# Head sums of the squared differential queries and keys: one plain fp32 matmul each, or two matmuls of a rounded and a low part

## The chip, the cores and the metric

The kernel runs on one core of a Trainium2 chip. The metric is the device time of one execution in microseconds, the median of several runs. TensorE (PE) does the matmuls, VectorE (DVE), ScalarE (ACT) and GpSimd (POOL) the elementwise work; SyncE (SP) starts most of the DMAs. Every engine works through its own list in a fixed order and waits on semaphores.

## What is computed

Two transformer blocks follow each other on a sequence of 512 tokens of width 1024. The change lies in the second block, in its differential attention. There queries and keys are normalised head by head before the scores:

```python
q, k, v = jnp.split(z.astype(F32), 3, axis=-1)
q = rms_normalize(q.reshape(B, S, H, 2, DIFF_QK)) * q_norm.astype(F32)
k = rms_normalize(k.reshape(B, S, H, 2, DIFF_QK)) * k_norm.astype(F32)
```

`rms_normalize` divides by the root of the mean of the squares over the 64 elements of a half head (plus 1e-6). Queries and keys together are 1024 columns: eight tiles of 128 columns by 512 tokens, with two half heads in each tile. In the same block stand a pooling mixer, an RWKV-7 mixer, then an output projection, a cross attention and a gated FFN.

## The kernel before, in words

Activations lie transposed, features on the partitions and the 512 tokens along the free axis. Every large projection is written as three matmuls in a rounded format (fp32r): ACT rounds the weights of a chunk of 256 output columns to a high part (L1192, one instruction of 128x2048 per chunk), POOL subtracts to get the low part (L2499, four instructions of 128x512), and PE adds high x high, high x low and low x high (`mm3`, eight contraction steps, so 24 matmuls for a tile of 128x512). The activations are split in the same way into `h_high_low` and `h_low`. The constants lie in `consts`; `blk` there is a 128x128 matrix with 1/64 in its two diagonal 64x64 blocks, so that a matmul with it gives each row the mean over its half head.

The stage around the change treats eight tiles t = 0 to 7 (`dq`, four of queries and four of keys). For each tile:

- PE projects it (`project("dq", ...)`) into a bank of PSUM.
- DVE multiplies by the token scale and writes it to `dqk`, which is `xres` (`dq_out`, L2095).
- ACT squares it into `qk_sq`, one of two buffers in `sums` (`dq_square`, L1579).
- PE forms the means, `dq_sum(t)`, through the helper `block_sum`: one plain fp32 matmul of 128x512 with `blk`. The profile shows a plain fp32 matmul as two instructions ("x2"), so the four for two tiles read "banks<-sums,consts ... x4".
- ACT takes Ln and Exp(-0.5 x) of it (`dq_inverse`, L1585 and L1587). From t = 2 on it first waits until the DVE has scaled tile t - 2, which used the same buffer (`dqk_ready` at least t - 1).
- DVE multiplies by gain and inverse (`dqk_scaled`, L2168), which counts `dqk_ready` up.

Each engine's order is written out by hand. PE: dq 0 to 3 with other small sums between (kk, pool, bonus), sums 0 and 1, dq 4, sums 2 and 3, dq 5, sum 4, dq 6, sum 5, dq 7, sum 6, sixteen transposes (nat 0, into four banks), sum 7, sixteen transposes (nat 1), then the value projection `dv` (128x256 tiles). All of these results pass through a ring of four banks, and `take` waits until the former tile of a bank has been moved out. DVE: `dq_out(3)`, two products from PSUM (`bonus`, L2178), `decayed(0)` (six operations, L2114 to L2120), `dq_out(4)`, `dqk_scaled` 0 and 1, `decayed(1)` (the same six lines), `dq_out(5)`, `dqk_scaled(2)`, `dq_out(6)`, `dqk_scaled(3)`, `dq_out(7)`, `dqk_scaled` 4 to 7. ACT: after `dq_square(7)` it does `dq_inverse(6)`, moves the four nat 0 banks (L1238), does `dq_inverse(7)` and moves the four nat 1 banks. Rounding the weights of the first `dv` chunk (L1192) stands behind `dq_square(5)`.

The means over all features of a token (`norm_sum`) and the sums kk and bonus are plain fp32 matmuls as well and are not touched. `nF_rows` (tile `forget_rows`) and `masks` hold data of the first block's attention; `nF_rows` is used again for the differential attention's outputs later.

Of the kernel before, what the change touches and what calls it, by code (L numbers as in the profile page):

```python
# [8 lines left out]
F32R = mybir.dt.float32r  # L9
BF16 = mybir.dt.bfloat16  # L10
ACT = mybir.ActivationFunctionType
ALU = mybir.AluOpType

P = 128
# [129 lines left out]
def build(nc, x_in, mem_in, params_in, consts_in, ada_in, stream_in, with_f_in, down_in, out, x2_kept, kx_kept, vx_kept, nF_kept, sums_kept):  # L144
    with ExitStack() as ctx:
# [3 lines left out]
        def sem(name):  # L149
            if name not in sems:  # L150
                sems[name] = ctx.enter_context(nc.semaphore(name))
            return sems[name]
# [62 lines left out]
        def sb(name, *dims, kind=F32):  # L215
            n = int(np.prod(dims))
            return view(ctx.enter_context(nc.sbuf_tensor(name, [P, n], kind))[:, :], dims)
# [13 lines left out]
        xres = sb("xres", KD, T)  # L231
        h_raw, h_lo = sb_both("h", KD, T)
        h_high, h_hi = sb_both("h_high", KD, T)
        sums = sb("sums", 4, T)
        sq, acc, rms = sums[:, 0:2, :], sums[:, 2, :], sums[:, 3, :]
        mod = sb("mod", 24)
        gmod = sb("gmod", 8)
        gmix = sb("gmix", 8)
        small = sb("small", 64)
        dq8 = sb("dq8", 2)  # L240
        masks = sb("masks", 3, P, kind=BF16)
        nF_rows = sb("forget_rows", 2, T)

        with nc.sbuf_tensor("arena", [P, ARENA], F32) as arena:
            pass
# [66 lines left out]
        POOL_W = PAD + T  # L312
        ycat03 = at(5152, 4, T)
        dqk = xres
        qk_sq, qk_rinv = sq, [acc, rms]
        zscale, rms2 = at(23456, T), sq[:, 1, :]

        dv, dist = zm[:, 0:4, :], zm[:, 4:8, :]
# [165 lines left out]
        def _(pe):  # L484
# [304 lines left out]
            def block_sum(key, j, src, ready):  # L789
                pe.wait_ge(sem(ready), j + 1)  # L790
                o = M.take(pe, (key, j))
                mm(o, blk, src, True, True, M.filled)

            def dq_sum(t):
                block_sum("dn", t, qk_sq[:, t % 2, :], "qk_squares")

            project("zr", 1, KD, h, T, first=5)
            rates(0)
# [360 lines left out]
        def _(act):  # L1159
# [13 lines left out]
            def split_weights(part=0, parts=1):  # L1173


                c = chunks[0]
                if part == parts - 1:
                    chunks[0] += 1
                if c >= STREAM:
                    down_high(c - STREAM)  # L1180
                    return
                n = width_of(c) // parts
                cols = slice(n * part, n * (part + 1))
                if part == 0:
                    act.wait_ge(*loaded_of(c))
                    if hi_holder(c) is not None:
                        end = chunk_end[hi_holder(c)]
                        if end[0] == "used":
                            act.wait_ge(used[end[1]], end[2])
                        else:  # L1190
                            full(end)
                nc.scalar.activation(hi_of(c)[:, cols], raw_of(c)[:, cols], ACT.Copy)\  # L1192
                    .then_inc(sem("weights_hi"), PIECES // parts)
# [324 lines left out]
            squares(3, xres, T, lambda k: act.wait_ge(sem("x2_ready"), k + 1))  # L1518

            act.dma_start(x2_kept, xres).then_inc(sem("x2_stored"), 16)  # L1520
            split_weights()
            inverse_rms(3, T, rms2)

# [51 lines left out]
            def dq_square(t):  # L1575
                if t >= 2:
                    M.full(act, ("dn", t - 2))
                M.wait_out(act, ("dq", t))
                nc.scalar.activation(qk_sq[:, t % 2, :], dqk[:, t, :], ACT.Square).then_inc(sem("qk_squares"), 1)  # L1579

            def dq_inverse(t):
                o = M.full(act, ("dn", t))
# [248 lines left out]
        def _(dve):  # L1831
# [280 lines left out]
            def decayed(j):  # L2112
                dve.wait_ge(sem("kk_norm"), j + 1)
                link(tt(adec[j], adec[j], tB[j], ALU.mult))  # L2114
                link(tt(bdec[j], avec[j], adec[j], ALU.mult))
                dve.wait_ge(sem("exps"), 4 * j + 4)
                tt(rdec[j], rdec[j], zm[:, j, :], ALU.mult).then_inc(sem("decayed"), 1)
                tt(bdec[j], bdec[j], kdec[j], ALU.mult).then_inc(sem("decayed"), 1)
                tt(kdec[j], kdec[j], kvec[j], ALU.mult).then_inc(sem("decayed"), 1)
                stt(adec[j], adec[j], -1.0, decay[j], ALU.mult, ALU.mult).then_inc(sem("decayed"), 1)  # L2120
# [22 lines left out]
            def dq_out(t):  # L2143
                token_scaled(("dq", t), dqk[:, t, :])

            inv_count = con("inv_count", 2, T)
            for j in range(2):
# [14 lines left out]
                    ins = tt(d, d, u[rows, PAD:], ALU.subtract)  # L2162
                ins.then_inc(sem("pooled"), 1)

            def dqk_scaled(t):
                dve.wait_ge(sem("qk_inverse"), t + 1)
                g = dq8[:, 0:1] if t < 4 else par("dk_g")
                stt(dqk[:, t, :], dqk[:, t, :], g, qk_rinv[t % 2], ALU.mult, ALU.mult).then_inc(sem("dqk_ready"), 1)  # L2168

            dq_out(1)  # L2170
            for j in range(2):
                o = M.full(dve, ("kk", j))
                ts(tB[j], o, float(HEAD), 1e-24, ALU.mult, ALU.max).then_inc(M.out(("kk", j)), 1)
            dq_out(2)
            dq_out(3)
            for j in range(2):
                o = M.full(dve, ("bonus", j))
                stt(bonus[j], o, float(HEAD), zm[:, 4 + j, :], ALU.mult, ALU.mult).then_inc(M.out(("bonus", j)), 1)  # L2178
            decayed(0)
            dq_out(4)  # L2180
            dqk_scaled(0)
            dqk_scaled(1)
            decayed(1)
            dq_out(5)
            dqk_scaled(2)
            dq_out(6)
            dqk_scaled(3)
            dq_out(7)
            for t in range(4, 8):
                dqk_scaled(t)  # L2190

# [551 lines left out]
```

## Time and profile before

| | |
|---|---|
| median of 3 runs | 1288.5 us (1288.05 to 1291.14) |
| the profiled execution | 1291.47 us, span from first to last instruction 1289.7 us |
| PE busy | 1253.3 us, 97% of the span |
| DVE, ACT, POOL busy | 699.2, 568.5 and 530.7 us |
| mean granted TensorE clock | 0.997 |
| stage of the change | about 582 to 642 us of the span |

How to read it: times are microseconds from the span's start. A row of a timeline has the start, the duration, the engine and line, the operation, the tiles it writes and reads, how many instructions are merged, and in brackets how long the engine was idle before and what released it. A merged row's duration runs from the first start to the last end. Matmuls are pipelined, so a fp32r matmul of 128x512 is shown with 0.39 or 0.40 us although the next one starts 0.23 us later; the pace is read from the starts.

### The profile page before, as it was taken

What the parts mean: (1) busy time and instruction counts of PE and PEld (TensorE: products, weight loads), DVE (VectorE), ACT (ScalarE), POOL (GpSimd) and SP (SyncE); (2) the same over time, 40 slices, a digit from 0 to 9 for tenths busy, and PEclk for the clock granted to TensorE, in tenths of its full rate; (3) what the DMA queues carried; (4) which work ended last, traced back from release to release, by engine and by line L of the source; (5) the groups of instructions that cost most, each with busy time, mean ns of one, the idle gap of its engine ahead of it and who ended that gap; (6) DMA issues with size and microseconds to landing.
All of it is one profiled execution on the core that took longest, in us unless ns stands there. A gap on an engine that the chain in (4) does not pass through costs nothing.

```text
span 1289.7 us, 20794 instructions
## 1 busy us (share of the span) xinstructions
PE 1253.3 (97%) x8570; PEld 1019.5 (79%) x8570; DVE 699.2 (54%) x1093; ACT 568.5 (44%) x870; POOL 530.7 (41%) x424
## 2 busy tenths in 40 slices
PE   6999999999999999999998899999999999999999
PEld 5788888866678888767786767788788888888999
DVE  3250004886431266686557657265565665766773
ACT  6541444786665233354544544353422221224452
POOL 6544454322234544534242126331444444546321
PEclk9999999999999999999999999999999999999999
DMA  9836795612115452412220013310222222224554
GB/s 387 348 131 243 248 230 191 163 50 97 51 66 188 122 163 79 181 66 76 69 107 16 3 66 131 135 61 34 99 98 98 81 87 94 99 88 172 166 185 151
DMA packets 24907, 165.05 MB, mean 128 GB/s; under 512 B 2792, under 2 KB 2920, under 8 KB 11504
## 3 DMA queue, kind: packets, MB, share of 16 engines
q1 hardware_dynamic: 20448, 128.15, 27.9%
q10 hardware_dynamic: 2064, 24.07, 5.0%
q0 software_dynamic: 2304, 11.54, 4.5%
q8 instruction: 68, 1.11, 0.3%
q14 instruction: 23, 0.19, 0.0%
HBM read 157.43 MB, written 29.38 MB: 145 GB/s over the span
## 4 chain that ended last, share of the span: by engine, by line
PE 89%; DVE 4%; ACT 3%; POOL 2%; issue 1%; DMA 0%; SPq 0%; DVEq 0%; ACTq 0%
PE banks L488 87%; PE banks L495 2%; DVE arena L1985 1%; POOL h_low L2557 1%; DVE arena L1982 1%; DVE arena L1987 1%; POOL weights_low L2557 1%; DMA arena<-in_mem 0%; ACT weights_high L1192 0%; ACT arena L1238 0%; ACT memory_high L1248 0%; ACT arena L1416 0%; ACT arena L1417 0%; ACT arena L1415 0%; DVE arena L1943 0%
## 5 line engine op out<-in xcount | busy, mean ns | idle before, releaser
L2499 POOL TENSOR_TENSOR weights_low<-weights,weights_high 128x512 fp32r<-128x512 f32 x324 | 433.2, 1367 | 580.5 <-ACT weights_high L1192 580.5
L488 PE MATMUL banks<-h_high_low,weights_high 128*128 128x512 f32 x880 | 358.2, 407 | 1.6 <-ACT arena L1443 1.6
L488 PE MATMUL banks<-h_low,weights_high 128*128 128x512 f32 x880 | 348.9, 397 | 0.0
L488 PE MATMUL banks<-h_high_low,weights_low 128*128 128x512 f32 x880 | 348.8, 396 | 0.0
L1192 ACT ACTIVATE weights_high<-weights 128x2048 fp32r<-128x2048 f32 (+2 forms) x90 | 156.3, 1737 | 243.1 <-PE banks L488 226.0
L488 PEld LDWEIGHTS banks<-h_high_low,weights_high 128*128 128x128 f32 x880 | 166.0, 189 | 46.0 <-issue 5.8
L488 PEld LDWEIGHTS banks<-h_low,weights_high 128*128 128x128 f32 x880 | 166.0, 189 | 41.8 <-issue 3.6
L488 PEld LDWEIGHTS banks<-h_high_low,weights_low 128*128 128x128 f32 x880 | 165.8, 188 | 40.4
L488 PE MATMUL banks<-arena 64*64 64x64 f32 (+6 forms) x1800 | 118.1, 263 | 4.1 <-issue 2.6
L488 PEld LDWEIGHTS banks<-arena 64*64 64x64 f32 (+3 forms) x1800 | 85.9, 148 | 29.9 <-issue 23.2
L1238 ACT ACTIVATE arena<-banks 128x256 f32<-128x256 f32 (+4 forms) x82 | 41.9, 519 | 53.4 <-PE banks L495 35.1
L2411 DVE TENSOR_TENSOR arena<-banks,sums 128x512 f32<-128x512 f32 x22 | 15.2, 692 | 78.1 <-PE banks L488 73.0
L488 PE MATMUL banks<-t_high,weights_low 128*128 128x256 f32 x198 | 55.6, 281 | 0.0
L488 PE MATMUL banks<-weights_high,h_high_low 128*128 128x256 f32 (+1 forms) x192 | 55.3, 288 | 0.3 <-ACT arena L1238 0.3
L488 PE MATMUL banks<-weights_high,h_low 128*128 128x256 f32 (+1 forms) x192 | 54.2, 282 | 0.0
L488 PE MATMUL banks<-weights_low,h_high_low 128*128 128x256 f32 (+1 forms) x192 | 54.1, 282 | 0.0
L1221 ACT ACTIVATE sums<-xres 128x512 f32<-128x512 f32 x32 | 20.2, 631 | 70.3 <-DVE xres L2065 39.3
L1938 DVE COPY arena<-banks 128x256 f32<-128x256 f32 (+3 forms) x40 | 25.3, 632 | 47.1 <-PE banks L488 46.2
L488 PE MATMUL banks<-t_high,weights_high 128*128 128x256 f32 x154 | 43.5, 283 | 2.5 <-issue 1.5
L488 PE MATMUL banks<-t_high,h_high_low 128*128 128x256 f32 x154 | 42.7, 277 | 0.0
L2557 POOL TENSOR_TENSOR weights_low<-weights,weights_high 128x384 fp32r<-128x384 f32 (+1 forms) x20 | 21.3, 1094 | 47.3 <-ACT weights_high L1202 47.3
L495 PE MATMUL banks<-consts,arena 128*128 128x128 f32 x245 | 37.2, 277 | 1.6 <-DVE arena L2222 0.8
(360 smaller groups left out, 2371.9 us busy)
## 6 DMA issues: line engine op xcount, KB each, us to landing
weights<-in_stream SPq DMA_DIRECT2D x82, 1024.0 KB, 4.8
sums_kept<-in_down POOLq DMA_DIRECT2D x16, 704.0 KB, 12.8
arena<-in_ada SPq DMA_DIRECT2D x8, 1024.0 KB, 11.9
weights<-in_down SPq DMA_DIRECT2D x9, 704.0 KB, 4.1
weights<-sums_kept SPq DMA_DIRECT2D x9, 704.0 KB, 4.0
sums_kept<-in_down ACTq DMA_DIRECT2D x2, 2816.0 KB, 21.4
sums_kept<-sums_kept ACTq DMA_DIRECT2D x2, 2816.0 KB, 12.6
h<-sums_kept SPq DMA_DIRECT2D x7, 704.0 KB, 4.2
```

The source lines that it names most:

```text
L488: ins = nc.tensor.matmul(o, lhsT, rhs, start=start, stop=stop, skip_group_check=skip)
L495: ins = nc.tensor.transpose(o, i, ident[0:rows, 0:rows])
L1192: nc.scalar.activation(hi_of(c)[:, cols], raw_of(c)[:, cols], ACT.Copy)\
L1221: nc.scalar.activation(SQ[n][i % 2][:, 0:width], src[:, k, 0:width], ACT.Square)\
L1238: nc.scalar.activation(dst, s_, ACT.Copy).then_inc(ring_.out(key), 1)
L1938: nc.vector.tensor_copy(dst, o if src is None else src(o)).then_inc(ring_.out(key), 1)
L1982: link(stt(w, o[:, :, 0:end], 0.0, w, ALU.max, ALU.add))
L1985: ins = nc.vector.tensor_tensor_scan(v, ones(end), v, 0.0, ALU.mult, ALU.add)
L1987: tt(w, o[:, :, 0:end], w, ALU.subtract).then_inc(M2.out(("a", i)), 1)
L2411: tt(a[:, 2:T + 2], o, rms[:, :], ALU.mult).then_inc(M.out(("up", m, 0)), 1)
L2499: nc.gpsimd.tensor_tensor(lo_of(c)[:, cols], raw_of(c)[:, cols], hi_of(c)[:, cols].bitcast(F32), ALU.subtract).then_inc(sem("weights_split ...
L2557: nc.gpsimd.tensor_tensor(down_lo(i)[:, cols], down_raw(i)[:, cols], down_hi(i)[:, cols].bitcast(F32), ALU.subtract).then_inc(sem("down_lo ...
```

## The change

Each square is taken twice by ACT: once in fp32 (`qk_sq`) and once rounded to fp32r (`qk_hi`, in `nF_rows`). DVE subtracts the rounded one from the full one (`square_low`, writing `qk_lo` over `qk_sq`), and PE adds two fp32r matmuls with a fp32r copy of `blk` (`blk_r`, in the place of `masks`). `dq_sum` now waits for `qk_low`. Where the DVE does its eight subtractions is part of the diff. ACT makes `blk_r` once, between the second block's first norm and the next rounding of weights.

```diff
-        sums = sb("sums", 4, T)
+        sums, sums_r = sb_both("sums", 4, T)
...
-        masks = sb("masks", 3, P, kind=BF16)
-        nF_rows = sb("forget_rows", 2, T)
+        with nc.sbuf_tensor("masks", [P, 3 * P], BF16) as held:
+            pass
+        masks, blk_r = view(held[:, :], (3, P)), sb("blocks", 3 * P // 2, kind=F32R)[:, 0:P]
+        nF_rows, nF_rows_r = sb_both("forget_rows", 2, T)
...
-        qk_sq, qk_rinv = sq, [acc, rms]
+        qk_sq, qk_lo, qk_hi, qk_rinv = sq, sums_r[:, 0:2, :], nF_rows_r, [acc, rms]
...
+            pe.wait_ge(sem("blocks"), 1)
+
             def dq_sum(t):
-                block_sum("dn", t, qk_sq[:, t % 2, :], "qk_squares")
+                pe.wait_ge(sem("qk_low"), t + 1)
+                o = M.take(pe, ("dn", t))
+                mm(o, blk_r, qk_hi[:, t % 2, :], True, False)
+                mm(o, blk_r, qk_lo[:, t % 2, :], False, True, M.filled)
...
             act.dma_start(x2_kept, xres).then_inc(sem("x2_stored"), 16)
+            high(blk_r, blk, sem("blocks"))
             split_weights()
...
                 nc.scalar.activation(qk_sq[:, t % 2, :], dqk[:, t, :], ACT.Square).then_inc(sem("qk_squares"), 1)
+                nc.scalar.activation(qk_hi[:, t % 2, :], dqk[:, t, :], ACT.Square).then_inc(sem("qk_squares"), 1)
...
+            def square_low(t):
+                dve.wait_ge(sem("qk_squares"), 2 * t + 2)
+                low(qk_lo[:, t % 2, :], qk_sq[:, t % 2, :], qk_hi[:, t % 2, :], sem("qk_low"))
...
             dq_out(2)
+            square_low(0)
             dq_out(3)
+            square_low(1)
             for j in range(2):
                 o = M.full(dve, ("bonus", j))
                 stt(bonus[j], o, float(HEAD), zm[:, 4 + j, :], ALU.mult, ALU.mult).then_inc(M.out(("bonus", j)), 1)
             decayed(0)
+            square_low(2)
             dq_out(4)
+            square_low(3)
             dqk_scaled(0)
             dqk_scaled(1)
             decayed(1)
+            square_low(4)
             dq_out(5)
             dqk_scaled(2)
+            square_low(5)
             dq_out(6)
             dqk_scaled(3)
+            square_low(6)
             dq_out(7)
+            square_low(7)
             for t in range(4, 8):
                 dqk_scaled(t)
```

## Rows read from the trace of the kernel before

**Rows 1.** The page: span, TensorE's busy time, shares of the chain that ended last.
```profile
span 1289.7 us, 20794 instructions
PE 1253.3 (97%) x8570; PEld 1019.5 (79%) x8570; DVE 699.2 (54%) x1093; ACT 568.5 (44%) x870; POOL 530.7 (41%) x424
...
PE 89%; DVE 4%; ACT 3%; POOL 2%; issue 1%; DMA 0%; SPq 0%; DVEq 0%; ACTq 0%
```
**Rows 2.** Timeline of PE around sums 0 to 3 and dq 4.
```profile
607.96 1.88 PE L488 MATMUL banks<-sums,consts 128*128 128x512 f32 x4
...
609.91 0.39 PE L488 MATMUL banks<-h_low,weights_high 128*128 128x512 f32 x1
...
615.29 1.88 PE L488 MATMUL banks<-sums,consts 128*128 128x512 f32 x4
...
617.24 0.40 PE L488 MATMUL banks<-h_low,weights_high 128*128 128x512 f32 x1
```
**Rows 3.** ACT's rows of the stage: two squares, then tile 7 and the bank moves.
```profile
611.51 1.14 ACT L1579 ACTIVATE sums<-xres 128x512 f32<-128x512 f32 x2
...
636.54 0.63 ACT L1579 ACTIVATE sums<-xres 128x512 f32<-128x512 f32 x1 [3.39 <-DVE xres L2095]
637.20 0.69 ACT L1585 ACTIVATE sums<-banks,consts 128x512 f32<-128x512 f32 x1
...
638.46 2.04 ACT L1238 ACTIVATE arena<-banks 128x512 f32<-128x512 f32 x4
```
**Rows 4.** Instructions of `low` and `high` (min/median/max ns, first and last start).
```profile
L1855 DVE TENSOR_TENSOR gated_low<-arena,gated_high_a x4: 681/684/686, 390.0 to 391.8; 128x512 fp32r<-128x512 f32 x4
...
L1211 ACT ACTIVATE masks<-consts x3: 304/308/309, 78.5 to 78.9; 128x128 bf16<-128x128 f32 x3
```
**Rows 5.** Timeline of DVE, from `dq_out(3)` to `dq_out(4)`.
```profile
606.44 0.69 DVE L2095 TENSOR_TENSOR xres<-banks,arena 128x512 f32<-128x512 f32 x1 [6.64 <-PE banks L488]
...
608.16 0.69 DVE L2178 SCALAR_TENSOR_TENSOR arena<-banks,arena 128x512 f32<-128x512 f32 x1 [0.17 <-PE banks L488]
608.77 1.55 DVE L2114 TENSOR_TENSOR arena<-arena 128x512 f32<-128x512 f32 x1
...
615.95 0.68 DVE L2120 SCALAR_TENSOR_TENSOR arena<-arena 128x512 f32<-128x512 f32 x1
616.55 0.68 DVE L2095 TENSOR_TENSOR xres<-banks,arena 128x512 f32<-128x512 f32 x1
```
**Rows 6.** Timeline of POOL from 608 to 617 us.
```profile
608.51 6.37 POOL L2499 TENSOR_TENSOR weights_low<-weights,weights_high 128x512 fp32r<-128x512 f32 x4 [9.61 <-ACT weights_high L1192]
```
**Rows 7.** Timeline of PE from sum 6 to the first matmul of `dv`.
```profile
635.55 1.02 PE L488 MATMUL banks<-sums,consts 128*128 128x512 f32 x2
636.41 2.18 PE L495 MATMUL banks<-consts,arena 128*128 128x128 f32 x16
639.18 1.10 PE L488 MATMUL banks<-sums,consts 128*128 128x512 f32 x2 [0.58 <-ACT arena L1238]
640.11 1.91 PE L495 MATMUL banks<-consts,arena 128*128 128x128 f32 x16
642.27 0.39 PE L488 MATMUL banks<-weights_high,h_high_low 128*128 128x256 f32 x1 [0.25 <-ACT arena L1238]
```
**Rows 8.** Timeline of DVE, scaling of tile 6 (`dqk_scaled(6)`).
```profile
638.58 0.75 DVE L2168 SCALAR_TENSOR_TENSOR xres<-xres,params,sums 128x512 f32<-128x512 f32 x1 [0.81 <-ACT sums L1587]
```
**Rows 9.** Busy time and granted clock (the number behind POOL) by stretch.
```profile
548.00:552.00 4.00, 1.09 (x6) 0.33 (x4) 3.85 (x7) 3.04 (x5) 0.00 (x0) 1.00 0.00 0
552.00:556.00 4.00, 4.00 (x9) 2.17 (x8) 3.84 (x6) 3.33 (x6) 0.00 (x0) 0.57 0.01 4
673.00:677.00 4.00, 2.39 (x76) 2.01 (x74) 2.48 (x9) 3.86 (x9) 1.26 (x1) 1.00 0.53 168
677.00:681.00 4.00, 3.70 (x182) 3.17 (x183) 3.47 (x9) 1.12 (x3) 0.89 (x1) 1.00 0.26 102
743.00:747.00 4.00, 4.00 (x18) 2.30 (x18) 3.49 (x5) 0.96 (x3) 3.65 (x3) 0.57 0.66 205
```

## The prediction

> **What bounds the kernel now.** I read the page first, then the timelines of PE, DVE, POOL and ACT for the stage of the change, and last the granted clock. PE is busy for 97% of the span and carries 89% of the chain that ended last [rows 1]. So a microsecond taken from PE's list is worth a microsecond, and a microsecond in which PE waits costs one. In the timelines the reader is to see two places of this stage where another engine runs beside PE with little or no slack: the DVE in `decayed(0)`, and ACT between tile 7's square and the bank moves.
>
> **What the change removes.** Sums 0 and 1 start at 607.96 us, and the second matmul of dq 4 starts at 609.91 us: 1.95 us for two sums and one fp32r matmul [rows 2]. The 23 fp32r matmuls from 609.91 to 615.29 us take 5.38 us, 0.234 us each. So a plain sum costs (1.95 - 0.23) / 2 = 0.86 us, and two fp32r matmuls of the same size cost 0.47 us. The saving is 0.39 us for a sum, 3.1 us for eight. If nothing else moved, this would be the gain.
>
> **What it adds and where that lies.** ACT gets eight more squares at a pace of 0.52 us (two take 1.14 us, one alone 0.63 [rows 3]). DVE gets eight subtractions; the same helper on the same shape and types takes 0.68 us [rows 4], at DVE's pace of 0.60 us from start to start [rows 5]. Both engines are idle for almost half of the kernel, so their busy time is nothing. What matters is that `dq_sum(t)` now stands behind a DVE instruction, in DVE's fixed order.
>
> *Sums 0 and 1.* `square_low(0)` waits only for ACT and is over before dq 3 ends. `square_low(1)` follows `dq_out(3)` at 606.44 us and ends near 607.8 us; PE wants it at 608.4 us. No wait. It pushes the products behind it by up to 0.6 us, but the second one waited for PE until 608.16 anyway [rows 5], so `decayed(0)` starts about 0.1 us later. PE gains 2 x 0.39: dq 4 starts 0.8 us earlier and ends at 615.29 - 0.77 = 614.5 us.
>
> *Sums 2 and 3.* This is the first stall. `square_low(2)` stands behind `decayed(0)`. That begins at 608.77 us and its last operation starts at 615.95 us; `dq_out(4)` follows at 616.55 us, not because PE was late (dq 4 ended at 615.3) but because the DVE was busy [rows 2, 5]. The reason is visible beside it: POOL's weight subtractions run from 608.51 us for 6.37 us [rows 6], and the first operation of `decayed(0)` takes 1.55 us, where the last takes 0.68 us [rows 5]. So `square_low(2)` starts at 616.65 us and ends at 617.35 us; PE, ready at 614.5 us, stands still for 2.9 us. Then sum 2 (0.47 us, to 617.9), while the DVE does `dq_out(4)` (from 617.25) and `square_low(3)` (617.86 to 618.56). PE waits another 0.7 us, does sum 3 and starts dq 5 at 619.1 us. Before, dq 5 started at 617.24 - 0.23 = 617.0 us [rows 2]. At this point the change has lost 2.1 us, the saving of four sums included.
>
> The Trainium skill ("SBUF — State Buffer", section "Who interferes with whom") says that a DVE instruction with two SBUF inputs contends with a GpSimd instruction that reads SBUF and that the loser waits for the whole instruction. By that rule `square_low(2)` itself, with two SBUF inputs, would also be slow if POOL were still at work; POOL has ended by 614.9 us [rows 6], so it would make no difference here, and the 1.55 us against 0.68 us agree with the rule.
>
> *Sums 4 to 6.* Sum 4 follows dq 5, which ends at 624.7 us. Behind sum 3 the DVE has two scalings and the six operations of `decayed(1)`, at 0.6 to 0.75 us each now that POOL is idle: from 618.5 us about 5.2 us. `square_low(4)` then ends near 624.4 us, just in time, with some 0.3 us to spare; were it late by 0.5 us, PE would lose 0.2. Sums 5 and 6 have a whole tile (5.6 us) between `dq_out` and their turn. They gain 3 x 0.39 for sums 4 to 6, of which the two before dq 7 ends put that end, E, at 636.9 us against 635.55 us: 1.3 us late.
>
> *Sum 7 and the transposes.* This is the second stall, and it is counted from E, because everything in it hangs on `dq_out(7)`. Before, PE was paced by ACT's moves from the transposes on: it waited 0.58 us before sum 7 and 0.25 us before `dv` [rows 7]. ACT squares tile 7 at E + 0.99 and starts Ln(6) at E + 1.65 [rows 3, 7]. From there ACT works without a gap: Ln, Exp, four moves of nat 0, Ln(7), Exp(7), first move of nat 1, and `dv` starts at 642.27 us, 5.07 us after Ln(6). Now Ln(6) must wait for `dqk_ready` of tile 4, and the DVE reaches `dqk_scaled(4)` only behind `square_low(7)`, which waits for both squares of tile 7. The sum: 0.99 + 1.14 (two squares) + 0.65 (the subtraction and its signal) + 0.75 (the scaling [rows 8]) + 0.1 (signals) = 3.6 us in place of 1.65. So `dv` starts at E + 8.7 in place of E + 6.7: 1.95 us lost, and the 0.39 us each that sums 6 and 7 save vanish in the wait. PE's share of it is one gap of about 2.9 us after the first sixteen transposes.
>
> *The copy of `blk`.* One ACT instruction of at most 0.3 us [rows 4] in front of a rounding of weights. At worst it passes to PE with 0.2 us; I take 0.1.
>
> Together: 1.3 + 1.95 + 0.1 = +3.4 us. The following stages are paced by PE and what follows from it, so I pass it on unchanged.
>
> **The clock.** Between 548 and 552 us PE is busy for 1.09 of 4 us, and in the following 4 us the mean granted clock is 0.57, that is mostly 1.2 GHz in place of 2.4; a second stretch of this depth lies at 743 to 747 us. Each takes 4 x 0.43 = 1.7 us from a PE that has work. Against it: from 673 to 677 us PE is busy for 2.39 of 4 us, and the clock stays at 1.00 then and after [rows 9]. The first new gap (2.9 us, 0.5 us of work, 0.7 us) is as deep as the one at 548; the second (2.9 us between transposes) is nearly so. If the clock falls behind the first, dq 5 pays 1.7 us in full. Behind the second, transposes and `dv` pay between 0.5 and 1.7 us; I take 1.3.
>
> The Trainium skill ("TensorE: Matmul & The Clock Gate", section "What's actually happening") says that TensorE's clock is gated to half unless recent activity has released it; the rows at 548 to 556 us agree. Without any such fall the time would be that of the third case below, 1291.9 us.
>
> **The cases.** The sum stands against the profiled span of 1289.7 us (1291.47 us with what lies around it); I add the difference to the median, 1288.5. A measurement of this kernel can't tell 0.3%, 3.9 us, from no change.
>
> - *One fall of the clock* (40%): 3.4 + 1.7 = +5.1, taken as 1293.6 us.
> - *Two falls* (27%): 3.4 + 1.7 + 1.3 = +6.4, 1294.9 us, at most 1.7 each, 1295.3 us.
> - *Only the stalls* (20%): +3.4, 1291.9 us, within 0.3%. For it: at 673 us PE lost 1.6 of 4 us and kept its clock. Against it: the new gaps are longer.
> - *Not slower* (10%): `square_low(2)` comes early. If POOL's subtractions fell outside `decayed(0)`, its six operations would take 4 us and end near 613 us, before PE asks. The first stall of 3.6 us is gone, what remains is -2.3 at E, +1.95 and 0.1: 1288.3 us. It decides from the point where POOL starts after about 613 us. Against it: POOL is released by ACT's rounding, which waits for the end of dq 3 and is not moved by the change. A second form, that later stages swallow the 3 us, ends at the same time.
> - *A true gain* (3%): no wait in either place, -3.1, 1285.4 us. It would need the order on DVE not to bind, and the DVE without a free moment from 608.16 to 616.55 us [rows 5] speaks against it.
>
> The likeliest is 1293.6 us, its own range 1292.5 to 1294.6. The range 1290.5 to 1296.0 takes in the first three cases with 0.7 us for the lengths of the DVE's slow operations, and leaves out the last two. Of the stalls-only case a part lies above 3.9 us and a part of the one-fall case below: slower 0.70, same 0.26, faster 0.04.
>
> **What the changed profile would show.** PE waits on the DVE's subtraction (L1855, `low`) at about 614.5 us for 2.9 us and once more for 0.7 us; sums 0, 1, 4, 5 and 6 start at once. The sums' pairs read fp32r tiles and take 0.47 us. Ln(6) on ACT waits for the DVE's scaling until about E + 3.6, and PE stands for about 2.9 us before sum 7. `dv` starts about 3.3 us late with the clock full, about 5 us with one fall. The clock would be near 0.5 for some 3.4 us behind 618 us or 643 us. The prediction is wrong if POOL's work is not beside `decayed(0)`, if `square_low(4)` misses dq 5's end by more than 1 us, or if neither gap costs clock.

## The result and the profile after

The changed kernel is slower: 1294.79 us (median of 6 runs, 1292.3 to 1296.79) against 1288.28 us, ratio 1.0044 with a 95% interval of 1.0034 to 1.0054. The forecast was 1293.6 us, with 1290.5 to 1296.0 as its range; the measured time is where the case of two falls of the clock was put (1294.9 us).

The page of the changed kernel: span and TensorE's busy time, to be held against [rows 1].

```profile
span 1295.0 us, 20811 instructions
...
PE 1253.8 (97%) x8570; PEld 1023.0 (79%) x8570; DVE 712.9 (55%) x1101; ACT 573.2 (44%) x879; POOL 532.7 (41%) x424
```

The span is 5.3 us longer and TensorE's busy time is almost the same. 3.1 us of matmul passes are gone from it and matmuls at the lower clock have taken their place; the span grew by waits. The timeline of PE in the stage of the change shows both (compare [rows 2, 7]):

```profile
606.92 1.88 PE L490 MATMUL banks<-arena,consts 128*128 128x512 f32 x4
608.23 0.80 PE L490 MATMUL banks<-forget_rows_low,blocks 128*128 128x512 f32 x1
...
617.99 0.50 PE L490 MATMUL banks<-forget_rows_low,blocks 128*128 128x512 f32 x1 [2.65 <-DVE sums_low L1864]
...
619.19 0.50 PE L490 MATMUL banks<-forget_rows_low,blocks 128*128 128x512 f32 x1 [0.48 <-DVE sums_low L1864]
...
639.09 0.39 PE L490 MATMUL banks<-forget_rows_low,blocks 128*128 128x512 f32 x1
...
639.54 1.47 PE L497 MATMUL banks<-consts,arena 128*128 128x128 f32 x12
643.44 0.66 PE L497 MATMUL banks<-consts,arena 128*128 128x128 f32 x4 [2.43 <-ACT sums L1594]
644.68 0.77 PE L490 MATMUL banks<-forget_rows_low,blocks 128*128 128x512 f32 x1 [0.58 <-ACT arena L1245]
645.25 0.63 PE L490 MATMUL banks<-sums_low,blocks 128*128 128x512 f32 x1
645.67 3.62 PE L497 MATMUL banks<-consts,arena 128*128 128x128 f32 x16
648.94 0.56 PE L490 MATMUL banks<-weights_high,h_high_low 128*128 128x256 f32 x1
```

The reader is to see the wait of 2.65 us ahead of sum 2 and 0.48 us ahead of sum 3, both released by the DVE's subtraction, and then 2.43 us inside the first batch of transposes, released by ACT. The last sixteen transposes take 3.62 us where they took 1.91 [rows 7]: the clock is down. The first row is the start of the bonus sums, 606.92 us here and 606.24 us before (the row below); I use it as the stage's zero, because the kernel's start alone differs between executions by up to 2 us. From it to the first matmul of `dv` the changed kernel takes 42.0 us and the kernel before 36.0 us.

```profile
606.24 1.88 PE L488 MATMUL banks<-arena,consts 128*128 128x512 f32 x4
```

The DVE of the changed kernel, where the first wait is made (compare [rows 5]):

```profile
609.52 1.51 DVE L2123 TENSOR_TENSOR arena<-arena 128x512 f32<-128x512 f32 x1
...
616.66 0.68 DVE L2129 SCALAR_TENSOR_TENSOR arena<-arena 128x512 f32<-128x512 f32 x1
617.26 0.68 DVE L1864 TENSOR_TENSOR sums_low<-sums,forget_rows_low 128x512 fp32r<-128x512 f32 x1
617.86 0.68 DVE L2104 TENSOR_TENSOR xres<-banks,arena 128x512 f32<-128x512 f32 x1
618.46 0.67 DVE L1864 TENSOR_TENSOR sums_low<-sums,forget_rows_low 128x512 fp32r<-128x512 f32 x1
```

ACT of the changed kernel behind dq 7 (compare [rows 3]): square and rounded square of tile 7, then Ln of tile 6 with 1.48 us of waiting for the DVE's scaling.

```profile
640.07 0.63 ACT L1587 ACTIVATE sums<-xres 128x512 f32<-128x512 f32 x1 [3.33 <-DVE xres L2104]
640.61 0.61 ACT L1588 ACTIVATE forget_rows_low<-xres 128x512 fp32r<-128x512 f32 x1
642.70 0.69 ACT L1594 ACTIVATE sums<-banks,consts 128x512 f32<-128x512 f32 x1 [1.48 <-DVE xres L2181]
...
643.96 2.04 ACT L1245 ACTIVATE arena<-banks 128x512 f32<-128x512 f32 x4
```

Stretches of the changed kernel (busy time of PE, PEld, DVE, ACT, POOL, then the granted clock):

```profile
614.00:619.00 5.00, 2.06 (x8) 1.05 (x6) 5.00 (x7) 0.00 (x0) 1.58 (x1) 1.00 0.00 0
619.00:625.00 6.00, 5.81 (x18) 4.62 (x19) 5.85 (x10) 3.56 (x6) 0.00 (x0) 0.72 0.00 0
638.00:643.00 5.00, 3.02 (x20) 2.42 (x18) 2.44 (x4) 1.45 (x3) 0.00 (x0) 1.00 0.49 151
643.00:652.00 9.00, 7.98 (x40) 7.47 (x41) 1.77 (x3) 8.17 (x13) 0.20 (x1) 0.62 0.26 84
```

Behind each wait the clock is at 1.2 GHz in place of 2.4 for a while, which is called a fall of the clock below: 6 x 0.28 = 1.7 us of full-speed time withheld behind the first wait, 9 x 0.38 = 3.4 us behind the second.

### The profile page after: what moved, and what is told of

Same layout as the page of the kernel before. It is cut to its first block, busy times and chain, and to the rows that moved or that the text cites. A ratio compares the mean times of both kernels' runs of the same rounds, so it can differ in the third digit from the quotient of the medians.

```text
span 1295.0 us, 20811 instructions
## 1 busy us (share of the span) xinstructions
PE 1253.8 (97%) x8570; PEld 1023.0 (79%) x8570; DVE 712.9 (55%) x1101; ACT 573.2 (44%) x879; POOL 532.7 (41%) x424
## 4 chain that ended last, share of the span: by engine, by line
PE 88%; DVE 5%; ACT 3%; POOL 2%; issue 1%; DMA 1%; SPq 0%; DVEq 0%; ACTq 0%
PE banks L490 86%; PE banks L497 2%; DVE arena L1994 1%; POOL h_low L2578 1%; DVE arena L1996 1%; DVE arena L1991 1%; POOL weights_low L2578 1%; DMA arena<-in_mem 1%; ACT weights_high L1199 0%; ACT memory_high L1255 0%; ACT arena L1423 0%; ACT arena L1424 0%; ACT arena L1422 0%; DVE arena L1952 0%; DVE arena L1947 0%
## 5 line engine op out<-in xcount | busy, mean ns | idle before, releaser
L490 PEld LDWEIGHTS banks<-arena 64*64 64x64 f32 (+3 forms) x1800 | 85.4, 147 | 29.3 <-issue 22.6
L1228 ACT ACTIVATE sums<-xres 128x512 f32<-128x512 f32 x32 | 20.2, 632 | 70.3 <-DVE xres L2074 39.3
```

The lines of the kernel that those rows point to most:

```text
L490: ins = nc.tensor.matmul(o, lhsT, rhs, start=start, stop=stop, skip_group_check=skip)
L1228: nc.scalar.activation(SQ[n][i % 2][:, 0:width], src[:, k, 0:width], ACT.Square)\
```

## The experiments

All but two start from the changed kernel; "before, gap at 548 filled" and "sums inside, plain" start from the kernel before. "Stage" is the time from the start of the bonus sums to the first matmul of `dv` in the profiled execution, E the end of dq 7 (the start of sum 6). The falls are those of this one execution too; the ratios are of 6 to 12 timed runs to the kernel before on the same chip.

| kernel | stage, us | bonus to E | E to dv | falls of the clock in the stage | ratio (95% interval) |
|---|---|---|---|---|---|
| before | 36.0 | 29.3 | 6.7 | none | 1 |
| changed | 42.0 | 32.2 | 9.9 | two | 1.0044 (1.0034 to 1.0054) |
| changed, again | 42.0 | 32.2 | 9.9 | two | 1.0046 (1.0031 to 1.0061) |
| gaps filled | 39.3 | 30.6 | 8.7 | none | 1.0041 (1.0028 to 1.0053) |
| gaps filled, again | 39.3 | 30.6 | 8.7 | none | 1.0047 (1.0034 to 1.0061) |
| no subtraction | 34.0 | 26.9 | 7.1 | none | 0.999 (0.9979 to 1.0001) |
| plain sums, same waits | 41.6 | 31.8 | 9.9 | one | 1.0041 (1.0028 to 1.0054) |
| scaling first | 39.2 | 32.2 | 7.1 | one | 1.0027 (1.0011 to 1.0042) |
| early subtractions | 39.0 | 30.3 | 8.7 | none | 1.0036 (1.0021 to 1.005) |
| POOL later | 38.4 | 29.0 | 9.4 | one | 1.0015 (1.0001 to 1.0028) |
| before, gap at 548 filled | 36.0 | 29.3 | 6.7 | none | 0.9989 (0.9977 to 1.0002) |
| sums inside | 33.8 | 27.1 | 6.8 | none | 0.9983 (0.9972 to 0.9994) |
| sums inside, gap at 548 filled | 33.8 | 27.1 | 6.8 | none | 0.999 (0.9979 to 1.0001) |
| sums inside, plain | 36.0 | 29.3 | 6.7 | none | 1.0001 (0.9991 to 1.0011) |

**1. What the matmuls alone are worth.** The subtraction is left out, and PE waits for ACT alone.

```diff
-                pe.wait_ge(sem("qk_low"), t + 1)
+                pe.wait_ge(sem("qk_squares"), 2 * t + 2)
...
-                mm(o, blk_r, qk_lo[:, t % 2, :], False, True, M.filled)
+                mm(o, blk_r, qk_hi[:, t % 2, :], False, True, M.filled)
...
-            square_low(0)
```

(and the other seven calls). Expected:

> The changed kernel without the DVE's eight subtractions: the second matmul of each sum reads the rounded squares again, so the means are not the right ones; PE waits for ACT's squares only. Theory: two fp32r matmuls are 0.39 us cheaper than a plain one, and what made the change slower is the place of the subtraction in the DVE's order. Then dq 5 starts about 1.5 us earlier than in the kernel before, dq 7 ends 2.3 us earlier, and the chain behind it (one more square on ACT, 0.52 us) leaves about -1.8 us: 1286.5 us. Rival: the loss is on ACT (more squares) or in the matmuls themselves: then the time stays above 1288.5 us.

Measured: 1287.75 us beside 1289.15 us. E comes 2.4 us earlier than before (six sums of 0.39 us), the rest 0.4 us later. The matmuls bring what the price said, ACT's second square costs 0.4 us, and neither is the loss. The timed gain is 1.4 us where 1.8 us was expected, and its interval (0.9979 to 1.0001) just takes in no gain at all.

**2. What the waits alone cost.** The plain matmul is back, subtraction and wait stay.

```diff
-                mm(o, blk_r, qk_hi[:, t % 2, :], True, False)
-                mm(o, blk_r, qk_lo[:, t % 2, :], False, True, M.filled)
+                mm(o, blk, qk_sq[:, t % 2, :], True, True, M.filled)
...
-                low(qk_lo[:, t % 2, :], qk_sq[:, t % 2, :], qk_hi[:, t % 2, :], sem("qk_low"))
+                low(qk_hi[:, t % 2, :], qk_sq[:, t % 2, :], qk_hi[:, t % 2, :], sem("qk_low"))
```

Expected:

> The changed kernel with the plain fp32 matmul back in each sum, reading the full squares; the second square, the subtraction (written over the rounded square) and PE's wait for it stay. Theory: the waits are anchored on the DVE, so most of the matmul's saving is lost in them anyway. Sum 3 starts when the changed kernel's does, dq 5 starts at +2.5 us to the kernel before in place of +2.1, dq 7 ends at +2.5, the second stall adds 1.95: +4.5 us with the clock full. With the same falls of the clock about 0.8 to 1.5 us above the changed kernel, near 1295.8 us. Rival: the saving of the matmuls counts in full, then 3.1 us above it, 1297.9 us.

Measured: 1294.4 us beside 1289.15 us, the same as the changed kernel (ratio 1.0041 and 1.0044), where 0.8 to 1.5 us more was expected. E is 2.4 us later than before, as expected (2.5), and only one fall of the clock lies in this profile's stage: behind the wait ahead of sum 2, 1.84 us here, the clock stayed up. The rival, that the saving counts in full, is out by 3.5 us.

**3. The DVE's order: two subtractions moved up.**

```diff
-            decayed(0)
+            decayed_first(0)
             square_low(2)
-            dq_out(4)
             square_low(3)
+            decayed_last(0)
+            dq_out(4)
```

(`decayed_first` holds the first two operations, `decayed_last` the other four.) Expected:

> The changed kernel with the subtractions of tiles 2 and 3 moved up on the DVE, behind the first two of the six operations of decayed(0). Theory: the DVE's list from decayed(0) to decayed(1) is full, so what binds is its total length and not the place of the two subtractions. Then PE's wait ahead of sum 2 vanishes (0 to 0.2 us in place of 2.65), dq 5 starts about 3 us earlier, and a new wait of about 3 us stands ahead of sum 4, whose subtraction follows decayed(1); dq 6 starts only 0.3 us earlier than in the changed kernel, and the time is about 1294.5 us. Rival: the place of the subtractions was the fault: then sum 4 waits for nothing and 2.5 to 3 us are won, 1291.5 to 1292 us.

Measured: 1294.72 us beside 1289.65 us. Timeline of PE:

```profile
613.86 0.40 PE L490 MATMUL banks<-forget_rows_low,blocks 128*128 128x512 f32 x1
...
614.89 0.50 PE L490 MATMUL banks<-forget_rows_low,blocks 128*128 128x512 f32 x1 [0.40 <-DVE sums_low L1864]
...
623.68 0.50 PE L490 MATMUL banks<-forget_rows_low,blocks 128*128 128x512 f32 x1 [2.44 <-DVE sums_low L1864]
```

The wait has gone from sum 2 to sum 4, hardly smaller, and E comes 0.3 us earlier than in the filled kernel of experiment 6, whose clock is full up to E as well. So the length of the DVE's list between `dq_out(3)` and `decayed(1)` binds, and not the place of two entries in it.

**4. POOL out of the DVE's way.**

```diff
                     n = width_of(c) // PIECES
+                    if c == chunk_end.index(("dq", 7)):
+                        pool.wait_ge(sem("decayed"), 8)
```

Expected:

> The changed kernel with POOL's four subtractions for the weights of dq 6 and 7 held back until decayed(1) is over, so that they don't run beside decayed(0). Theory: the first operations of decayed(0) take 1.5 to 1.8 us instead of 0.68 only because POOL reads SBUF beside them. Then each takes about 0.7 us, decayed(0) is over about 3.7 us after its start, sum 2 waits for nothing, and the first stall is at most 0.5 us; about 3 us won in the stage up to dq 5. Given back: the subtraction of tile 4 then meets POOL (up to 1 us), and the first piece of the weights may be late for dq 6 (up to 1.5 us). Time 1291.5 to 1293 us. Rival: the operations are slow for a reason of their own: then nothing changes ahead of sum 2, and dq 6 becomes late on top.

Measured: 1291.87 us beside 1289.65 us. The DVE in this kernel:

```profile
609.24 0.68 DVE L2123 TENSOR_TENSOR arena<-arena 128x512 f32<-128x512 f32 x1
...
612.49 0.68 DVE L2129 SCALAR_TENSOR_TENSOR arena<-arena 128x512 f32<-128x512 f32 x1
613.09 0.68 DVE L1864 TENSOR_TENSOR sums_low<-sums,forget_rows_low 128x512 fp32r<-128x512 f32 x1
```

With POOL starting at 621.63 us instead of beside it, `decayed(0)` starts its six operations within 3.3 us instead of 7.1; sum 2 waits for nothing, sum 3 for 0.92 us, and E comes 3.2 us earlier than in the changed kernel, 1.6 us earlier than in the filled one (below), whose clock is full as well. What is given back in between is sum 3's wait and 0.22 us for the late weights, and slower steps of dq 6. So the first wait is made by two engines reading SBUF side by side. The Trainium skill ("SBUF — State Buffer", section "Who interferes with whom") gives the rule, that a DVE instruction with two SBUF inputs contends with a GpSimd instruction that reads SBUF; this pair of runs agrees, 1.51 us against 0.68 us for the same instruction. In the run with the later POOL the slowness has moved along: the subtraction of tile 4, now beside POOL, takes 1.79 us.

**5. The second wait.**

```diff
+            dqk_scaled(4)
+            dqk_scaled(5)
             square_low(7)
-            for t in range(4, 8):
+            for t in range(6, 8):
                 dqk_scaled(t)
```

Expected:

> The changed kernel with the DVE's scaling of tiles 4 and 5 ahead of the subtraction of tile 7, nothing else. Theory: the second stall comes from ACT's Ln of tile 6, which waits for the scaling of tile 4 behind that subtraction. Then Ln(6) starts about 2.1 us after dq 7's end in place of 3.6, PE's gap in the transposes shrinks from 2.4 us to about 1 us, and with the gap goes the long fall of the clock behind it: 1.5 us plus 1.5 to 3 us, about 1291 us. Rival: the bank moves or sum 7 itself set the time there; then the time stays within 0.5 us of the changed kernel.

Measured: 1292.49 us beside 1289.15 us, 1.5 us above the expectation. E to `dv` is 7.1 us with the clock full there (1.6 us less than the 8.7 us of the filled kernel), and PE's wait in the transposes is 0.83 us. The wait was Ln(6)'s, through the scaling of tile 4. The stage shows this; the timed ratio (1.0011 to 1.0042) overlaps that of the changed kernel.

**6. The gaps filled with unread matmuls.**

```diff
+            def filler(n):
+                pe.wait_ge(moved[5], tiles[5])
+                for _ in range(n):
+                    mm(bank[5], blk_r, h_hi[:, 0, :], True, True)
...
             def dq_sum(t):
+                if t == 2:
+                    filler(11)
+                if t == 3:
+                    filler(2)
...
                 for i, src in enumerate((zm[:, 4 + j, :], kdec[j], bdec[j], adec[j])):
+                    if (j, i) == (0, 3):
+                        filler(10)
                     o = M.take(pe, ("nat", j, i))
```

Expected:

> The changed kernel with matmuls added that nobody reads: eleven of 128x512 (11 x 0.234 = 2.6 us) ahead of sum 2, two ahead of sum 3, ten ahead of the last four transposes of nat 0, all into an unused bank, each batch shorter than the gap in which it stands (2.65, 0.48 and 2.43 us of waiting in the changed kernel's profile, with the drain of the matmul before them). Theory: PE's waits cost about 3.4 us by themselves, and the rest, some 2 to 3 us, is the granted clock that falls to half behind either gap. Then the filled kernel keeps the waits' cost but not the falls: granted clock 1.00 from 610 to 655 us, time about 1292 us, 2 to 3 us under the changed kernel. Rival: the falls are no consequence of the gaps, or the whole loss is the waits: then the time stays at 1294.8 us or rises by what the fillers overrun, and the clock still falls near 620 and 645 us.

Measured: 1294.61 us beside 1289.15 us, 2.6 us above the expectation. PE and two stretches of the filled kernel (the first row is the start of the bonus sums, 636.89 us is E, the last row is `dv`):

```profile
606.26 1.88 PE L490 MATMUL banks<-arena,consts 128*128 128x512 f32 x4
...
614.52 2.68 PE L490 MATMUL banks<-h_high_low,blocks 128*128 128x512 f32 x11
617.35 0.50 PE L490 MATMUL banks<-forget_rows_low,blocks 128*128 128x512 f32 x1 [0.15 <-DVE sums_low L1875]
...
636.89 0.40 PE L490 MATMUL banks<-forget_rows_low,blocks 128*128 128x512 f32 x1
...
638.58 2.54 PE L490 MATMUL banks<-h_high_low,blocks 128*128 128x512 f32 x10
...
645.58 0.39 PE L490 MATMUL banks<-weights_high,h_high_low 128*128 128x256 f32 x1 [0.49 <-ACT arena L1256]
```

```profile
606.00:646.00 40.00, 38.63 (x176) 29.75 (x175) 27.73 (x34) 23.32 (x37) 11.92 (x8) 1.00 0.24 79
646.00:652.00 6.00, 6.00 (x52) 6.00 (x51) 0.00 (x0) 3.62 (x6) 3.13 (x3) 1.00 0.52 178
```

In the profile the theory holds: no fall, a stage 3.3 us longer than before, 2.7 us shorter than in the changed kernel. The timed runs don't show the 2.7 us. So both kernels were run once more, side by side on one chip:

> The changed kernel itself, once more, so that it is measured beside the filled one. Ratio to the kernel before 1.0035 to 1.0045 as at first; clock lower than in the kernel before by 0.001 to 0.002 on the mean over its runs.

> The changed kernel with filled gaps once more. Its first profile showed what the theory asks for (stage 3.3 us longer than before, clock full in it), its timed runs did not (5.3 us above the kernel before). If the clock's falls behind the new gaps are worth 2 us over many runs, it is now 1 to 2 us under the changed kernel of the same call. Rival: what the filled gaps save is lost to falls or waits in the later stages, and both are the same within 0.7 us.

Measured: changed 1296.07 us, filled 1294.68 us, beside 1288.76 us. The medians differ by 1.4 us, as the theory asked, but the ratios are the same, 1.0046 and 1.0047. Over all runs (12 each) the means are 1295.0 and 1294.7 us, a difference of 0.3 us with an uncertainty of about 1.5 us either way, and the mean clocks 0.9953 and 0.9972. So the full 2.7 us isn't borne out in the time; the runs can't tell a gain of 1 us from none. The stages of the second profiles repeat those of the first (42.02 and 39.3 us).

**7. The kernel before with its own gap filled.**

```diff
             project("zr", 1, KD, h, T, first=5)
+            pe.wait_ge(moved[7], tiles[7])
+            for _ in range(11):
+                mm(bank[7], h_hi[:, 0, 0:P], h_hi[:, 0, :], True, True)
             rates(0)
```

Expected:

> The kernel before, with eleven fp32r matmuls of 128x512 that nobody reads in its own gap of 2.9 us at 548 us (11 x 0.234 = 2.6 us, into an unused bank). Theory: the granted clock falls behind that gap because PE stood still, at a cost of up to 1.7 us, in part of the runs. Then the clock is 1.00 from 548 to 560 us and the time falls by 0.5 to 1.5 us, to about 1288 us, with fewer slow values. Rival: what a fall costs there is hidden, because ACT and the DVE set the pace behind the gap: then the clock is full but the time is the same as before within 0.3 us.

Measured: 1289.01 us beside 1289.65 us, ratio 0.9989 (0.9977 to 1.0002), mean clock 0.9989 over its runs against 0.9975. One stretch of it, to be held against [rows 9]:

```profile
544.00:560.00 16.00, 15.59 (x63) 10.65 (x63) 13.71 (x20) 10.60 (x16) 3.99 (x4) 1.00 0.20 67
```

The clock stays up where the kernel before lost it. What the fall there costs can be read from the first matmul behind the gap to the bonus sums: 55.0 us in the kernel before, 53.4 us in this one, and 53.4 us as well in the changed kernel's profile, which has the same gap unfilled and no fall behind it. So a fall costs 1.6 us at this place. The rows of that matmul in the kernel before, this one and the changed kernel, and the stretch behind it in the changed kernel:

```profile
551.24 0.70 PE L488 MATMUL banks<-arena,params 64*128 64x512 f32 x2 [2.91 <-issue]
```

```profile
550.88 0.70 PE L488 MATMUL banks<-arena,params 64*128 64x512 f32 x2 [0.41 <-issue]
```

```profile
553.51 0.70 PE L490 MATMUL banks<-arena,params 64*128 64x512 f32 x2 [2.91 <-issue]
```

```profile
553.50:560.00 6.50, 6.49 (x26) 4.39 (x27) 5.90 (x9) 5.23 (x8) 0.00 (x0) 1.00 0.45 155
```

In the timed runs the gain, if any, is under what they resolve.

**8. A better order.** PE does sums 2 to 5 inside the following projection, the DVE does the end of `decayed(1)` later and the scalings earlier, ACT does Ln and Exp of tile 6 ahead of the squares of tile 7.

```diff
-            for t in range(4, 8):
-                project("dq", 1, KD, h, T, first=t)
-                if t == 4:
-                    dq_sum(2)
-                dq_sum(t - 1)
+            project("dq", 1, KD, h, T, first=4)
+            inside = {5: {4: 2, 7: 3}, 6: {4: 4}, 7: {4: 5}}
+            for t in range(5, 8):
+                project("dq", 1, KD, h, T, lambda k: dq_sum(inside[t][k]) if k in inside[t] else None, first=t)
...
+            dq_sum(6)
...
-            dq_square(7)
             dq_inverse(6)
+            dq_square(7)
...
             dqk_scaled(1)
-            decayed(1)
+            decayed_first(1)
             square_low(4)
             dq_out(5)
             dqk_scaled(2)
             square_low(5)
+            decayed_last(1)
             dq_out(6)
             dqk_scaled(3)
             square_low(6)
+            dqk_scaled(4)
             dq_out(7)
+            dqk_scaled(5)
             square_low(7)
```

(The numbers by which the other engines wait for a full bank are adapted to the order in which the banks fill; `dqk_scaled` 6 and 7 follow.) Expected:

> The changed kernel in another order. PE does sums 2 and 3 inside the projection of dq 5 (ahead of its contraction steps 4 and 7), sum 4 inside dq 6 and sum 5 inside dq 7 (ahead of step 4). The DVE does the last four operations of decayed(1) behind the subtraction of tile 5, scales tile 4 ahead of dq_out(7) and tile 5 ahead of the subtraction of tile 7. ACT does Ln and Exp of tile 6 ahead of the squares of tile 7. Theory: with PE at work while the DVE catches up, no wait is over 0.5 us until the transposes, dq 7 ends 2 us earlier than in the kernel before, dv starts about 6.8 us behind it, so the stage is about 2 us shorter than before and the clock stays up in it: about 1287.2 us, 0.1 to 0.2% under the kernel before and 7 us under the changed one. Rival: the DVE or ACT is too full for any order: then a wait of 1 to 3 us stands ahead of sums 4 to 6, and the time is above 1289 us.

Measured: 1288.06 us beside 1289.65 us, ratio 0.9983 (0.9972 to 0.9994). All of PE's waits in its stage (engine, who released it, us in total, times, longest):

```profile
PE banks L490 <- DVE sums_low L1869: 1.4, 1, 1.4
PE banks L490 <- ACT arena L1250: 0.5, 1, 0.5
```

The stage is 2.2 us shorter than before, as expected, and this version beats both kernels, the kernel before by 0.17%. Whether the order or the matmuls did it is told by the same order with the plain sum, without second square, subtraction and copy:

```diff
-                pe.wait_ge(sem("qk_low"), t + 1)
-                o = M.take(pe, ("dn", t))
-                mm(o, blk_r, qk_hi[:, t % 2, :], True, False)
-                mm(o, blk_r, qk_lo[:, t % 2, :], False, True, M.filled)
+                block_sum("dn", t, qk_sq[:, t % 2, :], "qk_squares")
```

> The same new order with the plain fp32 matmul, no second square, no subtraction and no copy of blk: the order alone. Theory: the kernel before had no wait in this stage to gain from ahead of the transposes, so the order alone is worth only the 0.3 us at the transposes, and the gain of the new order with two matmuls is the matmuls' own: stage 35.8 us long (before 36.0, with two matmuls 33.9), time within 0.1% of the kernel before. Rival: the new order is what made that version fast: then this one is as fast or faster, 1287.5 us.

Measured: 1289.18 us beside 1288.76 us, ratio 1.0001, stage 36.0 us. The order alone gives nothing; the gain is the matmuls', which the first order had hidden behind the waits. Last, the better order with the gap at 548 us filled as in 7:

> The order with the sums inside the projections (run before this one) and in addition the eleven unread matmuls in the gap at 548 us. If both gains are real and independent: stage of the change 2.2 us shorter than in the kernel before, and the clock full at 552 us (up to 1.7 us): 0.2 to 0.3% under the kernel before, about 1286.8 us against 1289.7. Rival: the filled gap gives nothing beyond chance, because falls come elsewhere instead: then 0.15 to 0.2%, as without it.

Measured: 1288.01 us beside 1288.76 us, ratio 0.999 (0.9979 to 1.0001), where 0.2 to 0.3% was expected. The filled gap adds nothing that can be measured. With the same stage of 33.8 us these runs put the gain of the new order at 0.1%, with an interval that just takes in none; the 0.17% above is to be read with that.

## Why the prediction was right, and where it was not

*The price of the matmuls* (0.86 against 0.47 us) was right: experiment 1 puts six of them at 2.4 us.

*Sums 2 and 3* were right: expected 2.9 us (counted from the end of the matmuls' issue) and 0.7 us of standing, and a loss of 1.3 us at E. The filled kernel, whose clock is full, has it: 30.63 us from the bonus sums to E against 29.31 us. Sum 4 was right too: in the filled kernel its subtraction ends at 624.28 us and PE comes to it at 624.73 us, 0.4 us to spare where 0.3 was forecast. The cause is the one named, the full DVE list (experiment 3) made long by POOL beside it (experiment 4).

*Sum 7 and the transposes.* The size was right: Ln(6) starts 3.61 us after E in the changed kernel (3.6 expected), and E to `dv` is 8.7 us where the clock is full (8.7 expected). The place was wrong. "One gap of about 2.9 us after the first sixteen transposes" overlooked that the thirteenth transpose already needs the bank of sum 6, which Ln(6) frees. PE stands for 2.43 us there and for 0.58 us ahead of sum 7.

*The copy of `blk`* took 0.29 us on ACT. I had let 0.1 us pass to PE. It lies at 534.5 us. From PE's 2501st matmul, well ahead of it, to the bonus sums it is 187.6 us with the copy (changed kernel) and without it (before, gap filled), with no fall in between in either profile. So it costs PE nothing that shows, and the 0.1 us of the sum wasn't there.

*The clock* was the term that I sized too small. Both gaps brought a fall, in both profiles of the changed kernel; the likeliest case had one. Behind the first it cost 1.5 us (32.17 against 30.63 us from the bonus sums to E; 1.7 expected). Behind the second 1.3 us was expected and 1.7 the most; the fall lasts longer than any in the kernel before and costs 1.15 us up to `dv` (9.85 against 8.70 us) and 0.8 us more in the first twenty matmuls of `dv` (3.3 against 2.5 us), 2.0 us together. Taken together the profile's stage is 6.0 us longer, 3.3 for the waits and 2.7 for the clock. The span grew less, by 5.3 us: the changed profile starts 1.5 us later and is another 0.8 us late soon after, has no fall at 552 us (1.6 us back), and is 1.4 us shorter behind the start of `dv`.

*Luck.* The medians differ by 6.5 us and the case of two falls said 6.4, but that is closer than the working deserves. The second fall was sized too small, the sum knew nothing of the fall at 552 us that is missing or of the shorter rest, and these nearly cancel. Nor do all runs have both falls: those two withhold 1.7 + 3.4 = 5.1 us, which is a clock of 0.996, and three of the twelve runs of the changed kernel have 0.997 or more.

*What stays open.* By the stage alone, filling the gaps should have given back 2.7 us, and 12 runs on either side give 0.3 us, give or take 1.5. A part is seen in the profiles: both filled ones have the fall at 552 us, both changed ones don't, so that from the first matmul to `dv` they differ by 1.1 us only (634.1 and 635.1 against 635.5 and 635.9 us; the kernel before 630.3). That fall lies ahead of the fillers and is no work of theirs. Of the twelve profiles that have the gap of 2.91 us at 549 to 552 us unfilled, seven show a fall behind it and five don't (changed twice, scaling first, no subtraction, and sums inside, plain). In the five PE goes on 540.1 to 540.5 us after its first matmul, in the others at 539.0 to 539.8 us and once at 540.8 us. So where the same gap happens to lie in an execution goes with whether it costs clock. The three profiles with a wait of 2.65 us ahead of sum 2 and no filler (changed twice, scaling first) all belong to the five. Whether that wait also brings a fall in an execution of the other kind no profile shows. This could be why the fillers gave so little; it was not tested.

The clock of each timed run of the experiments is on record, and it gives an estimate. Within one kernel on one chip, over 198 runs in 16 sets, the time rises by 0.71 us (give or take 0.10) for each us of full-speed time withheld, that is the time multiplied by 1 less the clock. Carried to full clock at this rate, in the runs on one chip, the changed kernel is 3.2 us above the kernel before, which is what its waits say (3.3), and the other 3.4 us of the difference of the means are clock. The no-subtraction kernel comes out 1.8 us below (2.0 in the stage), sums inside 2.3 below (2.2), sums inside, plain 0.1 below (0.1). The kernels with unread matmuls fit worst, and all to the same side: the filled kernel is 4.8 and 5.4 us above where its stage says 3.3, sums inside with the filled gap 0.9 below (2.2), the kernel before with its gap filled 0.3 above (0.0). Each figure has an uncertainty of about 1 us. Either the unread matmuls cost something outside the stage, or the falls that they prevent are cheaper than the average one; no run tells these apart. So the share of the clock in the measured difference stays an estimate; the share of the waits, 3.3 us, is shown.

*The rivals.* "Not slower" named the right lever: with POOL away from `decayed(0)` E comes 0.3 us earlier than in the kernel before (2.3 in the forecast, which let no work of POOL meet the DVE later); it is still 0.15% slower, because the second wait is left and with it, in this profile, a fall of the clock. "A true gain" needs another order and is then there, 2.2 us in the stage.

## What to carry to other kernels

A cheaper instruction on the bounding engine is worth its price only if what it now waits for comes from an engine with room at that moment. Here TensorE's work got 3.1 us cheaper and the stage 3.3 us longer by waits alone, because eight short subtractions went into a list on the DVE that was full for almost 18 us, although the DVE is idle for 45% of the span. Look for what runs beside the new instruction, place the consumer later (inside the next projection) instead of the producer earlier, and ask which bank, buffer or scaling the delayed instruction frees further down.

## What the runs showed of the hardware

- The granted clock can stay at half for 6.8 us: in both profiles of the changed kernel it does, in the first from 644 us on at 0.50, where in the kernel before each fall took about 3.4 us. Transposes slow down with it (sixteen in 3.62 us against 1.91 us).
- A gap of the same length doesn't always bring a fall. The same wait of 2.91 us at the same place of the program had one behind it in seven profiles and none in five, and where it came it cost 1.6 us. So a few profiles don't say what length of gap is harmless: 2.65 us ahead of sum 2 brought the clock down in three profiles of three, 2.44 us ahead of sum 4 left it at 1.00 in one.
- Keeping TensorE busy with unread matmuls held the clock up and did not measurably shorten the kernel: the mean clock rose from 0.9953 to 0.9972 and the mean time stayed within 0.3 us, give or take 1.5.
- A DVE instruction of 128x512 that reads two SBUF tiles took 0.68 us with POOL idle and in most cases 1.5 to 1.8 us beside POOL's subtractions.
